# Fetched rows treated one by one, from dot to diagonal, outside the attention heads and the tanh units

## The chip, the cores and the metric

The kernel runs on one core of a Trainium2 chip. The metric is device microseconds of one execution. TensorE multiplies, VectorE and ScalarE work elementwise and reduce, GpSimd issues the gathers and SyncE the plain transfers; each engine works through its own list in order and waits on semaphores for the others.

## What is computed

Two blocks of a language model over 256 tokens of width 1024, in float32. The change is in the second block, whose two layers each end in a PEER feed-forward. It picks, for every token, 8 heads x 16 experts of 16384, and reads for each pick a row u and a row v:

```python
def peer_ffn(h, w_q, sub_keys, u_tab, v_tab):
    ...
    eidx = (i1 * PEER_NKEYS + i2).reshape(T, PEER_HEADS * PEER_TOPK)
    gates = jax.nn.softmax(cv, axis=-1).reshape(T, PEER_HEADS * PEER_TOPK)
    ...
        uc = jnp.take(u_tab, ic, axis=0)
        vc = jnp.take(v_tab, ic, axis=0)
        act = jax.nn.gelu(jnp.einsum('cd,ckd->ck', xc, uc).astype(jnp.float32))
        return jnp.einsum('ck,ckd->cd', (gc * act).astype(vc.dtype), vc)
```

Around it stand an LRU block, a stick-breaking attention with 16 heads, a per-layer embedding and norms. The first block (dilated attention, 32 experts of 2048 columns) comes before all that.

## The kernel before

The first 1165 us or so are the first block and the LRU block, most of it a stream of expert weights. Then the **row stage** begins. Layer by layer and token tile by token tile (128 tokens) it runs four **phases** f = 0 to 3: the PEER of layer 0 for tiles 0 and 1, then of layer 1 for both. A phase is 128 fetched "rows": row k holds, for each of the 128 tokens (one per partition), the u and v vectors of its k-th pick, 2 x 1024 floats, 1.05 MB in all. A phase has 64 **ticks** t of SHARE = 2 rows, a unit is one head of one tile (16 rows, 8 ticks).

The way of a row, with the lines of the profile:

- GpSimd issues its gather (L2701) into one of 8 buffers (9 from row 168 on), after it waited until TensorE had used the row that lay there before (`rows_used`). Indices come from the choice of the unit (`idx_ready`).
- VectorE multiplies u with the token vector in PSUM and sums (the dot, L2483), when the row has landed.
- ScalarE applies Gelu to the dots of the tick (L1871; in units 3 and 4 of phases 1 and 2 a Tanh form instead, L1869, `by_tanh`).
- VectorE multiplies it with the softmax factor into coefficients (L2510, tanh form L2507).
- ScalarE scales an identity by each coefficient into a diagonal (L1877, 8 slots).
- TensorE multiplies the diagonals with v into PSUM (`picks`, L1357) and so frees the row.

On every engine a tick is followed by a piece of other work, `chain(f - 1, t)`: the rest of the layer for the tile before (merging the sums at t = 0, squares, roots and scaled copies at t = 1 and 8, a gate with Sigmoid at 6 and 7, keys and values from 9, queries from 17, the attention heads from t = 22 to 38, the output projection from MERGE = 39, the questions to the next PEER from 45). Between dot and coefficient VectorE also runs pieces of the choice of later units (`choose`, L2412 to L2458), four to a unit: two top-16 searches of keys, one of pairs, and the row numbers. After a unit's last piece ScalarE computes an Exp for it (L1857). Gelu, Exp, Sqrt and Sigmoid each need other tables on ScalarE, so between them stands an ACT_TABLE_LOAD.

In `parts(f, t)` the two rows of a tick go together: two dots, then one Gelu over both, one coefficient instruction over both, two diagonals. Only in the last tick of all do they go one by one.

Of the kernel before, what the change touches and what calls it, by code (L numbers as in the profile page):

```python
# [35 lines left out]
TT = T // P  # L36
# [32 lines left out]
SHARE = 2  # L69
SHARES = PTOP // SHARE  # L70
PHASES = 2 * TT
PHASE = PH * PTOP
TICKS = PHASE // SHARE
# [10 lines left out]
HEADS, GROUP, GROUPS = 22, 4, HEADS2 // 4  # L84
SOFT, LOGS, MASKED, SUMS, ARGUE, EXPS, CAUSAL, WEIGH, KEEP = 1, 2, 3, 3, 5, 5, 6, 6, 7
MERGE, ADD3, SQUARE3, SCALE3, TURN3, GAIN3 = 39, 43, 43, 44, 44, 45
# [4 lines left out]
LAST, LAST_PROJ = PHASES - 1, 40  # L91
# [78 lines left out]
def row_buffer(k):  # L170

    return k % ROWS if k < MORE_AT else (k - MORE_AT + ROWS) % (ROWS + MORE_ROWS)
# [7 lines left out]
def chosen(f, t):  # L180

    if f == 0:
        return [FIRST_CHOICES[t]] if t in FIRST_CHOICES else []
    now = [(PH * f + 2 + j // 4, j % 4) for j in range(24) if int(1.75 * j) == t]
    if f < PHASES - 1 and CHOOSE <= t < CHOOSE + 8:
        now.append((PH * (f + 1) + (t - CHOOSE) // 4, (t - CHOOSE) % 4))
    return now
# [6 lines left out]

def parts(f, t):

    return range(SHARE) if (f, t) == (LAST, TICKS - 1) else range(0, SHARE, SHARE)


def by_tanh(f, t):  # L200

    return 1 <= f <= TT and t // SHARES in TANH_UNITS


class Tally:
# [6 lines left out]
    def mark(self, ins):  # L212
        ins.then_inc(self.sem, 1)
        self.n += 1
        return self.n
# [4 lines left out]
    def link(self, ins):  # L220
        self.mark(ins)
        self.wait()
# [9 lines left out]
def program(nc, io, out):  # L232
    first = plan()
    slot, slot_loads, freed_by = ring_plan(first)
    with ExitStack() as ctx:
# [187 lines left out]
        def rows(n):  # L423

            b = row_buffer(n)
            if b < ROWS:
                return big[:, b * ROW:(b + 1) * ROW]
            return ring[:, CHAIN_RING:RING, :].rearrange("p k d -> p (k d)")

        def diagonal(n):  # L430

            return diag_at[:, n % DIAGS * SIDE:(n % DIAGS + 1) * SIDE]
# [9 lines left out]
        def tok_bank(f):  # L442

            return (6, 0, 2, 0)[f]
# [1047 lines left out]
        def _(act):  # L1492
# [366 lines left out]

            def share(f, t):  # L1860

                for i, begin in enumerate(parts(f, t)):
                    n = f * TICKS + t + i
                    k = (f * TICKS + t) * SHARE + begin
                    size = SHARE // len(parts(f, t))
                    act.wait_ge(S["dots_ready"], n + 1)
                    at = slice(k % PICKS, k % PICKS + size)
                    if by_tanh(f, t):
                        act.activation(acts[:, at], g_arg, ACT.Tanh, scale=GELU_SLOPE).then_inc(S["gelu_ready"], 1)  # L1869
                    else:  # L1870
                        act.activation(acts[:, at], dots[:, at], ACT.Gelu_apprx_tanh, scale=1.0 if f else r_tok)\  # L1871
                            .then_inc(S["gelu_ready"], 1)
                    act.wait_ge(S["coef_ready"], n + 1)
                    for k in range(k, k + size):
                        if k >= DIAGS:
                            act.wait_ge(S["rows_used"], k + 1 - DIAGS)
                        act.activation(diagonal(k), fold, ACT.Copy, scale=coef[:, k % PICKS:k % PICKS + 1])\  # L1877
                            .then_inc(S["diags_ready"], 1)
# [7 lines left out]
            for f in range(PHASES):  # L1886
                for t in range(TICKS):
                    share(f, t)
                    if f == 0 and SECOND_CHOICE.get(t) == 2:
                        exps(1)  # L1890
# [33 lines left out]
        def _(dve):  # L1924
# [64 lines left out]
            for g, w in enumerate(POOL_WINDOWS):  # L1989
                s = (s0, s1)[g % 2][:, g, PAD:E]  # L1990
# [469 lines left out]
            def choose(n, piece):  # L2460
                if piece < 2:
                    best_keys(n, piece)
                elif piece == 2:
                    best_pairs(n)
                else:
                    rows_of(n)

            def share(f, t):

                u = f * PH + t // SHARES  # L2470
                u16 = u % UNITS
                if t == 0:
                    dve.wait_ge(S["tok_ready"], f + 1)
                tok = ps[:, tok_bank(f):tok_bank(f) + 2, :].rearrange("p b d -> p (b d)")
                for i, begin in enumerate(parts(f, t)):
                    n = f * TICKS + t + i
                    first_row = (f * TICKS + t) * SHARE + begin
                    size = SHARE // len(parts(f, t))
                    at = slice(first_row % PICKS, first_row % PICKS + size)
                    for k in range(first_row, first_row + size):  # L2480
                        dve.wait_ge(rows_loaded[row_buffer(k)], 16 * ROW_COUNT[k])
                        r = rows(k)[:, 0:D]
                        ins = dve.scalar_tensor_tensor(r, r, 1.0, tok, op0=ALU.mult, op1=ALU.mult,  # L2483
                                                       accum_out=dots[:, k % PICKS:k % PICKS + 1])
                        if by_tanh(f, t):
                            mark(ins)
                    if by_tanh(f, t):
                        step.wait()
                        link(dve.scalar_tensor_tensor(g_arg, dots[:, at], GELU_CUBE, dots[:, at], op0=ALU.mult, op1=ALU.mult))
                        dve.scalar_tensor_tensor(g_arg, g_arg, 1.0, dots[:, at], op0=ALU.add, op1=ALU.mult)\  # L2490
                            .then_inc(S["dots_ready"], 1)
                    else:
                        ins.then_inc(S["dots_ready"], 1)
                    if t % SHARES == 0:
                        dve.wait_ge(S["cv_exp"], u + 1)
                        link(dve.reciprocal(p_rec[:, u16:u16 + 1], p_sum[:, u16:u16 + 1]))
                        if by_tanh(f, t):
                            link(dve.tensor_scalar(p_rec[:, u16:u16 + 1], p_rec[:, u16:u16 + 1], 0.5, None, ALU.mult))
                    if by_tanh(f, t):
                        mark(dve.scalar_tensor_tensor(g_rest, dots[:, at], p_rec[:, u16:u16 + 1], cv[:, at],  # L2500
                                                      op0=ALU.mult, op1=ALU.mult))
                    for which, piece in chosen(f, t):
                        choose(which, piece)
                    dve.wait_ge(S["gelu_ready"], n + 1)
                    if by_tanh(f, t):
                        step.wait()
                        dve.scalar_tensor_tensor(coef[:, at], acts[:, at], 1.0, g_rest, op0=ALU.add, op1=ALU.mult)\  # L2507
                            .then_inc(S["coef_ready"], 1)
                    else:
                        dve.scalar_tensor_tensor(coef[:, at], acts[:, at], p_rec[:, u16:u16 + 1], cv[:, at],  # L2510
                                                 op0=ALU.mult, op1=ALU.mult).then_inc(S["coef_ready"], 1)
# [143 lines left out]
            for f in range(PHASES):  # L2655
                for t in range(TICKS):
                    share(f, t)
                    if f == 0 and t in SECOND_CHOICE:
                        choose(1, SECOND_CHOICE[t])
                    if f == 0 and t == ADD_NEXT:  # L2660
                        add_recurrent(1)
                    if f == 0 and t == SUM_NEXT:
                        sum_blocks(FFN + 1)
                    if f == 0 and t == NORM_NEXT:
                        tile_norm(FFN + 1, lambda c: col("norm_ffn", c))
                    if f == LAST and t == LAST_MERGE:
                        keep_sums(f)
                    if f:
                        chain(f - 1, t)
# [101 lines left out]
```

## Time and profile before

| | us |
|---|---|
| median of 3 runs | 2641.99 (2637.86 to 2642.75) |
| profiled execution | 2641.29 |
| its span, first to last instruction | 2639.1 |
| TensorE busy | 2149.6 |
| VectorE busy | 1362.4 |
| ScalarE busy | 633.1 |
| GpSimd busy | 492.7 |

The span holds 33067 instructions and 1053.60 MB of DMA, on average 399 GB/s; the gathers of the row stage are 540.07 MB of it. In the groups below, a time after a bar is idle time of the engine before those instructions, with what ended it; in the timelines it stands in brackets.

### The profile page before, as it was taken

Reading aid. Unit: us, or ns where it says so; the run is one execution under the profiler, and the core shown is the slowest. Engines: PE = TensorE matmul, PEld = TensorE weight load, DVE = VectorE, ACT = ScalarE, POOL = GpSimd, SP = SyncE. Lnnn points to the kernel's source line nnn. Section 1 sums busy time; section 2 is a strip of 40 time slices with the busy share of each in tenths; the row PEclk is TensorE's granted clock in tenths of the full one; section 3 lists DMA queues with packets and bytes.
Section 4 is the critical chain, followed back from the end, with each engine's and each line's share of the span. In section 5 each row is a group of like instructions: output and inputs, shape, how many; then the busy total and the mean of one; then the engine's idle time right before and its main releaser. Section 6 shows DMA issues by size and latency. Waiting matters only on the chain.

```text
span 2639.1 us, 33067 instructions
## 1 busy us (share of the span) xinstructions
PE 2149.6 (81%) x12087; PEld 954.9 (36%) x12087; DVE 1362.4 (52%) x3702; ACT 633.1 (24%) x1521; POOL 492.7 (19%) x534
## 2 busy tenths in 40 slices
PE   8999999999999999997765579577678677565557
PEld 6633333333333334994421123125123235121112
DVE  3422222122222123777677777874675875587754
ACT  0411111111111111342222242431332442232212
POOL 1000000000000000013333333332333332233331
PEclk9999999999999999999987789889799899687789
DMA  7899999999999999859999999999999999999995
GB/s 254 357 407 429 429 428 429 428 425 430 428 429 429 428 428 372 292 196 414 420 419 421 420 419 393 420 419 417 420 419 417 405 400 417 419 402 421 421 421 226
DMA packets 134409, 1053.60 MB, mean 399 GB/s; under 512 B 15601, under 2 KB 16025, under 8 KB 44177
## 3 DMA queue, kind: packets, MB, share of 16 engines
q0 software_dynamic: 75104, 540.07, 49.7%
q1 hardware_dynamic: 59184, 511.98, 47.0%
q8 instruction: 70, 1.15, 0.2%
q14 instruction: 51, 0.41, 0.0%
HBM read 1050.92 MB, written 2.63 MB: 399 GB/s over the span
## 4 chain that ended last, share of the span: by engine, by line
PE 41%; DMA 39%; DVE 13%; ACT 3%; issue 3%; POOL 1%; SPq 0%; DVEq 0%; POOLq 0%; ACTq 0%
DMA big<-in_uv,small 22%; PE ps L884 15%; DMA big<-in_w_gate_up 14%; PE ps L1357 7%; DVE big L2483 5%; PE ps L1049 3%; PE ps L1161 3%; DMA ring<-in_uv,small 2%; PE ps L926 2%; PE ps L1175 2%; PE ps L867 1%; PE ps L712 1%; ACT small L1877 1%; DVE small L2416 1%; DVE small L2413 1%
## 5 line engine op out<-in xcount | busy, mean ns | idle before, releaser
L1357 PE MATMUL ps<-big,small 64*64 64x512 f32 x3776 | 595.6, 741 | 389.8 <-ACT small L1877 385.7
L2701 POOL DMA_INDIRECT big<-in_uv,small x473 | 445.3, 941 | 1987.4 <-DVE small L2458 1109.4
L2483 DVE SCALAR_TENSOR_TENSOR big<-big,ps 128x1024 f32<-128x1024 f32 x473 | 569.5, 1218 | 265.1 <-DMA big<-in_uv,small 259.9
L884 PE MATMUL ps<-big 128*64 128x512 f32 x2304 | 525.6, 599 | 26.2 <-DMA big<-in_w_gate_up 23.9
L1357 PEld LDWEIGHTS ps<-big,small 64*64 64x64 f32 x3776 | 148.1, 157 | 758.3 <-ACT small L1877 560.8
L884 PEld LDWEIGHTS ps<-big 128*64 128x64 f32 x2304 | 156.0, 137 | 333.3 <-issue 288.5
L1877 ACT ACTIVATE small<-small 128x64 f32<-128x64 f32 x512 | 150.3, 340 | 299.5 <-DVE small L2510 242.1
L2160 DVE COPY big<-ps 128x512 f32<-128x512 f32 x32 | 22.1, 692 | 381.3 <-PE ps L884 381.3
L1871 ACT ACTIVATE small<-small 128x2 f32<-128x2 f32 (+1 forms) x225 | 51.7, 230 | 593.8 <-DVE big L2483 513.8
L2146 DVE TENSOR_TENSOR big<-ps,big 128x256 f32<-128x256 f32 x64 | 27.2, 425 | 299.5 <-PE ps L908 299.5
L1049 PEld LDWEIGHTS ps<-hs,ring 128*128 128x128 f32 x1152 | 131.7, 193 | 17.9 <-issue 16.0
L1049 PE MATMUL ps<-hs,ring 128*128 128x128 f32 x1152 | 136.3, 278 | 0.0
L884 PE MATMUL ps<-ring,big 128*64 128x512 f32 x512 | 121.1, 600 | 9.3 <-DMA ring<-in_w_gate_up 8.1
L2510 DVE SCALAR_TENSOR_TENSOR small<-small 128x2 f32<-128x2 f32 (+1 forms) x225 | 49.6, 221 | 81.9 <-ACT small L1871 76.7
L1583 ACT ACTIVATE big<-big 128x256 f32<-128x256 f32 x64 | 26.7, 416 | 228.8 <-DVE big L2147 228.8
L1357 PE MATMUL ps<-ring,small 64*64 64x512 f32 x312 | 53.7, 743 | 32.8 <-ACT small L1877 32.7
L1591 ACT COPY big<-ps 128x512 f32<-128x512 f32 x32 | 18.7, 585 | 250.8 <-PE ps L884 250.8
L1161 PE MATMUL ps<-ring,xT 128*128 128x512 f32 x152 | 70.6, 606 | 0.1
L1303 PEld LDWEIGHTS ps<-xT,ring 128*128 128x128 f32 x512 | 60.1, 196 | 13.7 <-issue 11.3
L926 PE MATMUL ps<-small,big 64*128 64x256 f32 x512 | 63.9, 389 | 0.0
L1571 ACT COPY big<-ps 128x512 f32<-128x512 f32 x32 | 18.7, 585 | 188.1 <-PE ps L884 188.1
L1303 PE MATMUL ps<-xT,ring 128*128 128x128 f32 x512 | 63.2, 283 | 0.5 <-DMA ring<-in_peer_w_q 0.5
(403 smaller groups left out, 2300.4 us busy)
## 6 DMA issues: line engine op xcount, KB each, us to landing
big<-in_w_gate_up SPq DMA_DIRECT2D x80, 2048.0 KB, 22.7
big<-in_w_down SPq DMA_DIRECT2D x64, 2048.0 KB, 24.1
ring<-in_w_gate_up SPq DMA_DIRECT2D x32, 2048.0 KB, 26.2
hs<-in_w_gate_up SPq DMA_DIRECT2D x16, 2048.0 KB, 26.1
ring<-in_peer_w_q SPq DMA_DIRECT2D x48, 512.0 KB, 9.8
ring<-in_ple_w_gate SPq DMA_DIRECT2D x22, 512.0 KB
ring<-in_w_in SPq DMA_DIRECT2D x16, 512.0 KB, 8.1
ring<-in_a_w_in SPq DMA_DIRECT2D x16, 512.0 KB, 5.0
```

What stands on the lines that cost most here:

```text
L884: last = pe.matmul(ps[side * CAP:(side + 1) * CAP, bank + b, :], o, w[:, at:at + BANK], start=start, stop=stop, skip_group_check=True)
L926: last = pe.matmul(half(G_OUT, side * DT // 2 + c), m_y[at, c * P:(c + 1) * P], m_gateT[at, :], start=False, stop=True, skip_group_check=True)
L1049: last = pe.matmul(ps[:, bank + e // 4, (e % 4) * P:(e % 4 + 1) * P], w[:, e * P:(e + 1) * P], src(c)[:, tt * P:(tt + 1) * P], start=(c == ...
L1161: last = pe.matmul(ps[:, bank + z, :], src[:, blocks(c)], w[:, z * BANK:(z + 1) * BANK], start=(c == 0), stop=(c == DT - 1), skip_group_ch ...
L1175: last = pe.matmul(ps[:, bank + half_, :], src[:, blocks(c)], w[:, half_ * BANK:(half_ + 1) * BANK], start=(c == 0), stop=(c == DT - 1), s ...
L1303: last = pe.matmul(ps[:, A + e // 4, blocks(e % 4)], w[:, blocks(e)], hd[:, blocks(c)], start=(c == 0 and e % 4 == 0), stop=(c == DT - 1), ...
L1357: last = pe.matmul(ps[tokens_ if by_halves else at, bank, :], diagonal(k)[tokens_, :], rows(k)[tokens_, D + z * BANK:D + (z + 1) * BANK], ...
L1871: act.activation(acts[:, at], dots[:, at], ACT.Gelu_apprx_tanh, scale=1.0 if f else r_tok)\
L1877: act.activation(diagonal(k), fold, ACT.Copy, scale=coef[:, k % PICKS:k % PICKS + 1])\
L2483: ins = dve.scalar_tensor_tensor(r, r, 1.0, tok, op0=ALU.mult, op1=ALU.mult, accum_out=dots[:, k % PICKS:k % PICKS + 1])
L2510: dve.scalar_tensor_tensor(coef[:, at], acts[:, at], p_rec[:, u16:u16 + 1], cv[:, at], op0=ALU.mult, op1=ALU.mult).then_inc(S["coef_ready" ...
L2701: pool.indirect_dma_start(out=rows(k), out_offset=None, in_=io[f"uv{n // UNITS}"], in_offset=bass.IndirectOffsetOnAxis(ap=rows_at[:, at:at ...
```

## The change

`parts` gives single rows in every tick, except in the two places where it still gives a pair: the tanh units (ticks 24 to 39 of phases 1 and 2) and the ticks of the attention heads (22 to 38 of the same phases). So 36 ticks stay paired, and 219 that were paired are split (the last was split before). In a split tick the order on VectorE is dot, wait for the Gelu, coefficient, dot, pieces of choosing, wait for the Gelu, coefficient; the reciprocal of a unit's sum goes with its first row. ScalarE does Gelu and diagonal for one row, then for the other. The counters behind `dots_ready`, `gelu_ready` and `coef_ready` are now counted by `parts_before`.

```diff
 def parts(f, t):
 
-    return range(SHARE) if (f, t) == (LAST, TICKS - 1) else range(0, SHARE, SHARE)
+    alone = (f, t) == (LAST, TICKS - 1) or not (by_tanh(f, t) or 1 <= f <= TT and HEADS <= t < MERGE)
+    return range(SHARE) if alone else range(0, SHARE, SHARE)
...
+def parts_before(f, t):
+
+    return sum(len(parts(g, s)) for g in range(f + 1) for s in range(t if g == f else TICKS))
...
+                done = parts_before(f, t)
                 for i, begin in enumerate(parts(f, t)):
-                    n = f * TICKS + t + i
+                    n = done + i
...
-                    if t % SHARES == 0:
+                    if t % SHARES == 0 and i == 0:
                         dve.wait_ge(S["cv_exp"], u + 1)
                         link(dve.reciprocal(p_rec[:, u16:u16 + 1], p_sum[:, u16:u16 + 1]))
...
-                    for which, piece in chosen(f, t):
+                    for which, piece in chosen(f, t) if i == len(parts(f, t)) - 1 else ():
                         choose(which, piece)
                     dve.wait_ge(S["gelu_ready"], n + 1)
```

The `done` lines stand in `share` of ScalarE and of VectorE alike. DMA, GpSimd and TensorE code is not touched.

## Rows read from the trace of the kernel before

**Rows 1.** The page: busy time per engine, and GB/s in 40 slices of the span.

```profile
PE 2149.6 (81%) x12087; PEld 954.9 (36%) x12087; DVE 1362.4 (52%) x3702; ACT 633.1 (24%) x1521; POOL 492.7 (19%) x534
...
GB/s 254 357 407 429 429 428 429 428 425 430 428 429 429 428 428 372 292 196 414 420 419 421 420 419 393 420 419 417 420 419 417 405 400 417 419 402 421 421 421 226
```

**Rows 2.** Windows: length, busy us of the engines, TensorE clock, DMA share, GB/s.

```profile
1595.00:1630.00 35.00, 35.00 (x158) 13.13 (x155) 20.78 (x58) 9.36 (x25) 12.96 (x15) 1.00 0.96 371
2065.00:2160.00 95.00, 72.10 (x468) 29.61 (x468) 80.34 (x219) 40.83 (x86) 32.48 (x35) 0.91 0.99 396
2310.00:2355.00 45.00, 32.58 (x172) 10.57 (x174) 37.67 (x102) 18.76 (x44) 16.17 (x18) 0.92 1.00 392
```

**Rows 3.** Chain of waits, 1570 to 1650: start, length, what.

```profile
1595.37 3.63 PE ps L1175 x8
1599.00 1.88 PE ps L1357 x16
```

**Rows 4.** Groups of VectorE, ticks 1 to 16 of phase 3: busy, mean ns, idle before.

```profile
L2483 DVE SCALAR_TENSOR_TENSOR big<-big,ps 128x1024 f32<-128x1024 f32 x29 | 34.3, 1215 | 0.0
L2510 DVE SCALAR_TENSOR_TENSOR small<-small 128x2 f32<-128x2 f32 x16 | 3.7, 231 | 9.3 <-ACT small L1871 9.2
```

**Rows 5.** The dots' groups, windows 1247.5:1515.6, 1542.5:1580.3, 1922.1:1960.4, 2377.6:2508.7 (two).

```profile
L2483 DVE SCALAR_TENSOR_TENSOR big<-big,ps 128x1024 f32<-128x1024 f32 x102 | 123.2, 1218 | 56.9 <-DMA big<-in_uv,small 55.3 <-issue 1.3
...
L2483 DVE SCALAR_TENSOR_TENSOR big<-big,ps 128x1024 f32<-128x1024 f32 x10 | 12.2, 1219 | 11.4 <-DMA big<-in_uv,small 11.4
...
L2483 DVE SCALAR_TENSOR_TENSOR big<-big,ps 128x1024 f32<-128x1024 f32 x11 | 13.3, 1217 | 9.8 <-DMA big<-in_uv,small 7.2 <-issue 2.5
...
L2483 DVE SCALAR_TENSOR_TENSOR big<-big,ps 128x1024 f32<-128x1024 f32 x46 | 55.7, 1218 | 18.0 <-DMA big<-in_uv,small 17.9
...
L2483 DVE SCALAR_TENSOR_TENSOR ring<-ring,ps 128x1024 f32<-128x1024 f32 x6 | 7.3, 1218 | 3.3 <-DMA ring<-in_uv,small 3.3
```

**Rows 6.** Timeline of VectorE, a bare tick: start, length, operation.

```profile
2345.79 1.22 DVE L2483 SCALAR_TENSOR_TENSOR ring<-ring,ps 128x1024 f32<-128x1024 f32 x1
...
2346.93 1.22 DVE L2483 SCALAR_TENSOR_TENSOR big<-big,ps 128x1024 f32<-128x1024 f32 x1
...
2348.56 1.21 DVE L2483 SCALAR_TENSOR_TENSOR big<-big,ps 128x1024 f32<-128x1024 f32 x1
```

**Rows 7.** Timeline of VectorE, ScalarE, the tick after an Exp (phase 3, tick 6).

```profile
2325.11 1.21 DVE L2483 SCALAR_TENSOR_TENSOR big<-big,ps 128x1024 f32<-128x1024 f32 x1
...
2329.23 0.22 DVE L2510 SCALAR_TENSOR_TENSOR small<-small 128x2 f32<-128x2 f32 x1 [1.76 <-ACT small L1871]
...
2327.70 1.28 ACT L1871 ACT_TABLE_LOAD   x1
```

**Rows 8.** Timeline of VectorE and ScalarE, tick 1 of phase 3.

```profile
2302.27 1.21 DVE L2483 SCALAR_TENSOR_TENSOR big<-big,ps 128x1024 f32<-128x1024 f32 x1
...
2306.78 0.22 DVE L2510 SCALAR_TENSOR_TENSOR small<-small 128x2 f32<-128x2 f32 x1 [0.56 <-ACT small L1871]
...
2306.46 0.20 ACT L1871 ACTIVATE small<-small 128x2 f32<-128x2 f32 x1
```

**Rows 9.** Timeline of TensorE, the two rows of tick 0 of phase 3.

```profile
2295.64 1.98 PE L1357 MATMUL ps<-ring,small 64*64 64x512 f32 x8 [4.65 <-ACT small L1877]
2297.37 1.96 PE L1357 MATMUL ps<-big,small 64*64 64x512 f32 x8
```

**Rows 10.** Timeline of VectorE, the coefficient of tick 7 of phase 3.

```profile
2336.83 0.22 DVE L2510 SCALAR_TENSOR_TENSOR small<-small 128x2 f32<-128x2 f32 x1 [3.51 <-ACT small L1871]
```

**Rows 11.** Timelines of GpSimd and VectorE: fetch and dot of rows 419, 161.

```profile
2368.20 0.94 POOL L2701 DMA_INDIRECT big<-in_uv,small  x1 [0.82 <-PE ps L1357]
...
2380.09 1.22 DVE L2483 SCALAR_TENSOR_TENSOR big<-big,ps 128x1024 f32<-128x1024 f32 x1 [1.26 <-DMA big<-in_uv,small]
...
1602.36 0.94 POOL L2701 DMA_INDIRECT big<-in_uv,small  x1 [0.30 <-issue]
...
1611.22 1.22 DVE L2483 SCALAR_TENSOR_TENSOR big<-big,ps 128x1024 f32<-128x1024 f32 x1
```

More of the change, by code:

```diff
@@ L2474, in share @@
                 tok = ps[:, tok_bank(f):tok_bank(f) + 2, :].rearrange("p b d -> p (b d)")
+                done = parts_before(f, t)
                 for i, begin in enumerate(parts(f, t)):
-                    n = f * TICKS + t + i
+                    n = done + i
                     first_row = (f * TICKS + t) * SHARE + begin
```

## The prediction

> **What bounds the kernel now.** I read the page first, then the windows, then the waits of VectorE. TensorE is the busiest engine by its share and VectorE has half the span [rows 1], but the 40 slices say what sets the time: outside the stage change near slice 17 the DMA moves some 420 GB/s until the end [rows 1]. The second half reads 512 rows of 1.05 MB; while only they are read, one costs 1.05 MB / 421 GB/s = 2.49 us, a tick of two 4.98 us. So a change pays or costs only where the DMA runs dry. The windows show three such stretches [rows 2]: 1595:1630 at 371 GB/s, 2065:2160 at 396, 2310:2355 at 392. Against 420 they lose 35 x 49/420 = 4.1, 95 x 24/420 = 5.4 and 45 x 28/420 = 3.0 us, 12.5 in all: the most that a better flow of buffers could win. It runs dry because a row is fetched only when the buffer eight or nine rows back has been multiplied.
>
> The dry stretches have different limits. The first is TensorE: weights and rows alternate, 3.63 + 1.88 = 5.51 us for each tick with never a gap [rows 3]. The second lies in ticks 25 to 43 of phase 2, of which the change leaves 25 to 39 alone. The third is the start of phase 3, where VectorE never waits for a row in 16 ticks (idle before its dots 0.0, the 29 of [rows 4] and 3 more) but waits 9.3 us for ScalarE; those ticks take 75.2 us, 4.70 each. Elsewhere VectorE has room: ticks 13 to 63 of phase 0 hold 56.9 us of waiting for rows (1.1 a tick), ticks 17 to 42 of phase 3 hold 18.0 + 3.3 = 21.3 (0.82 a tick) [rows 5].
>
> **What the change adds to a tick.** The dots, the diagonals and the matmuls stay as many. Each of 219 ticks (256 less 36 paired ones and the last, already split) gains one Gelu and one coefficient, and VectorE, which works in order, now stands still for ScalarE after each row. The price is in one bare tick [rows 6]: dot to dot is 2348.56 - 2346.93 = 1.63 us when the Gelu and the coefficient lie between, and 1.14 when they don't (2346.93 - 2345.79). So **+0.49 us on VectorE**, choice or no choice: a piece of choosing covers only the second Gelu.
>
> After an Exp, ScalarE reloads its tables first: diagonals, load, Exp, load, Gelu [rows 7]. In the pair two dots cover part of it, and the coefficient comes 2329.23 - 2325.11 = 4.12 us after the first dot. Alone, ScalarE starts 0.24 sooner (one diagonal fewer), the first coefficient comes at 3.86, the second a dot and a Gelu later at 5.49: **+1.37**, one tick in seven. The Trainium skill (ScalarE: Activation LUTs, What ACT_TABLE_LOAD costs) gives 1283 ns for the load and 2.66 us for a switch with its drain; [rows 7] show the 1.28 and the coefficient already 1.53 after the load began, so no drain. By the page's figure these ticks would cost some 2.8 us more each; nothing below uses it.
>
> Ticks 1 and 8 of phases 1 to 3 are dearest: ScalarE squares a tile, loads Sqrt, loads Gelu, and its Gelu ends 4.39 us after the first dot started [rows 8]. Two dots and a piece of choosing hid all but 0.56. Alone, the first coefficient waits till 4.51, and the second dot and the choosing (the coefficient's 4.51 less those 0.56 and the first dot's 1.14: 2.8) follow it, the second coefficient at 7.48: **+2.97**. No DMA issue moves in any queue's order; GpSimd and SyncE keep theirs, and the DMA bytes are the same. Bounds for all this: below, the Gelus could be absorbed by waits for rows, 0; above, every addition in a stretch without such waits.
>
> **What it gives back.** The first row of a pair no longer waits for its fellow: it is freed a dot (1.14) and perhaps a choice (up to 3.1) sooner relative to VectorE. The second finds TensorE with one row less to do: 0.9 us at full clock, 1.7 where the granted clock is low, as at tick 0 of phase 3 (2297.37 - 2295.64 between the two rows [rows 9]). There the merge waits for both, so tick 1 starts about 1.85 us sooner. In steady flow this is nothing: the DMA is the limit.
>
> **Where it lands.** Phase 0: 0.49 a tick plus the dear ones is 0.62 on average, under the 1.1 of waiting; carried from tick to tick VectorE's delay stays under 2.5 us, and buffers go out earlier by as much: 0, bounds -1 and +2. Phase 2: ticks 5 to 9 wait 9.8 us for rows [rows 5] and swallow it; its dry stretch is in the paired ticks: 0, bounds 0 and +1.
>
> Phase 1, start: tick 1 costs 2.97, ticks 2 to 4 0.5 each; waits for rows, 11.4 us over ticks 5 to 9 [rows 5], take it back. Tick 8 again, then 9 and 10: VectorE's tick 10 ends 3.5 us late. The TensorE stretch after it starts less late, since one row of tick 10 is already multiplied (0.94 at full clock, half of 1.88) and the Gelu of the other hides under its choice: some +1.5, an estimate. From there each tick is 5.51 us of TensorE, with VectorE at 5.9 or less in front of it, so the delay stays. The DMA is dry there: **+1.5**, bounds 0 and +3.5.
>
> Phase 3, start: -1.85 at tick 0, +2.97 at tick 1, +0.5 in ticks 2 and 3; TensorE's stretch over ticks 3 to 5 starts 1.1 late. Tick 6 has the tables (+1.37). At tick 7 the coefficient waits 3.51 us for ScalarE's Sigmoids [rows 10]; the pair had both dots and a choice done by then, alone the second dot and the choice (2.9) come after it and tick 8 starts +5.0. Tick 8: +2.97, so +7.9 at tick 9. Four ticks of 0.49: +9.9 at tick 13, whose first row (number 410) is freed 9.5 late, and so row 419 is fetched 9.5 late. How much of this the DMA had in hand is in the lead from fetch to dot: 2368.20 to 2380.09 is 11.9 us for row 419; in the dry stretch of phase 1 one took 1602.36 to 1611.22 = 8.9 [rows 11]. So 3.0 was queue, and up to 6.5 is idle DMA; less, as that 8.9 had VectorE's dot before it back to back and the row may have lain there. I take **+5**, bounds +1 and +11 (the whole delay). After tick 16 VectorE needs 4.98 - 0.82 + 0.62 = 4.8 a tick, still under 4.98: it catches up slowly and costs nothing more. The tail, already row by row, gains at most 0.3.
>
> Sum: 1.5 + 5 + 0 + 0 - 0.3 = +6.2 us on the profiled execution's 2641.3 (span 2639.1, about 2 us around it): 2647.5; the median of the runs is 0.7 above that execution, so **2648**.
>
> **Rivals.** *Hidden* (0.2): the lead hides more and the earlier buffers pay for phase 1: 0 to +4, 2642 to 2646. For it: the DMA reads 1.01 busy around all three stretches [rows 2]. Against: the 75.2 us without one wait for a row [rows 4].
>
> *Faster* (0.12): rows freed singly refill the queue. Each dry stretch begins when the held buffers reach the limit; freed one row's read (2.49) sooner, it starts 2.5 later. In stretches one and three that is -5, with none of the VectorE delay: 2637; more than 12.5 can't come. It decides where tick 10 of phase 1 and tick 9 of phase 3 end no later than before. The Trainium skill (Perfetto Trace Analysis, Optimizing Scalar/DVE Operations) says as much: where these engines aren't saturated but cause bubbles elsewhere, breaking up instructions may let work finish sooner; the same section has grouping pay where an engine is saturated. By the busy share of 52% the first half would apply, by [rows 4] the second does at phase 3's start.
>
> *VectorE becomes the bound* (0.13): phase 3 never catches up until tick 43 and the whole 11 shows, phase 1 gives its 3.5 and phase 0 its 2: 2642 + 16.5 = 2658.
>
> *As forecast* (0.55): +3 to +10, 2645 to 2652.
>
> **Numbers.** 0.2% of this kernel, 5.3 us, is about what can be told from nothing. The forecast case lies above it some six times in ten (0.33) and the bound case adds 0.13: slower 0.46. Same: 0.2 and the forecast's other 0.22, 0.42. Faster 0.12. The range 2638 to 2658 leaves out most of the faster case and the upper half of the bound case, under 0.2; the likeliest case alone is 2645 to 2652.
>
> **What would show it.** Coefficients (L2510) about 444 instead of 225, at 0.22 us, and their wait for ScalarE from 77 us to over 150; the idle before dots falls by about the sum; first row's dot to second row's dot 1.63 in bare ticks. Tick 1 of phase 3 near 8.5 us long (was 5.5), tick 8 near 9. The window after 2310 drier than 392 GB/s and longer. Wrong if VectorE's late ticks leave that window's GB/s as it was, if TensorE's stretch in phase 1 starts on time, or if the granted clock moves with the finer matmuls.

## The result, and the profile after

The median of 11 runs after is 2647.43 us (2643.25 to 2652.68), beside 2640.22 us (2636.32 to 2642.75) for 11 runs of the kernel before. The ratio is 1.0028, 95% interval 1.002 to 1.0035: 7 us slower, where +6.2 and a time of 2648 were forecast. The profiled execution took 2644.37 us with a span of 2642.2; that is 3.1 below its kernel's median, while the profiled execution before (2641.29) is 1.1 above its own, so the two traces differ in length by less than the kernels do.

The page after: busy times, GB/s in 40 slices, and three groups (busy, mean ns | idle before them).

```profile
PE 2186.6 (83%) x12087; PEld 944.0 (36%) x12087; DVE 1399.7 (53%) x3921; ACT 706.1 (27%) x1740; POOL 495.0 (19%) x534
...
GB/s 261 366 427 428 429 428 428 428 421 429 428 429 429 429 428 368 256 225 419 421 420 421 421 415 384 421 419 417 421 417 409 408 406 417 418 368 414 421 421 236
...
L2491 DVE SCALAR_TENSOR_TENSOR big<-big,ps 128x1024 f32<-128x1024 f32 x473 | 573.3, 1216 | 132.2 <-DMA big<-in_uv,small 131.8
...
L1878 ACT ACTIVATE small<-small 128x1 f32<-128x1 f32 (+1 forms) x444 | 101.9, 230 | 477.7 <-DVE big L2491 438.4
...
L2518 DVE SCALAR_TENSOR_TENSOR small<-small 128x1 f32<-128x1 f32 (+1 forms) x444 | 97.3, 219 | 207.8 <-ACT small L1878 206.0
```

The dots' group of the page before, for its idle time.

```profile
L2483 DVE SCALAR_TENSOR_TENSOR big<-big,ps 128x1024 f32<-128x1024 f32 x473 | 569.5, 1218 | 265.1 <-DMA big<-in_uv,small 259.9
```

Lines have moved: the dot is L2491 (was L2483), the coefficient L2518 (L2510), the Gelu L1878 (L1871), the diagonal L1884 (L1877), the multiplication with v L1363 (L1357), the gather L2709 (L2701). There are 219 more Gelus and coefficients, VectorE waits 206 us for ScalarE, and its idle time before the dots of this group has fallen by 132.9 us, which is 0.61 a split tick. Nearly all of that came out of waits for the DMA. In the GB/s line [rows 1] the slice that stands out is the 36th: 368 instead of 402.

Windows after (columns as in rows 2): TensorE's stretch of phase 1, phase 2's dry stretch, the start of phase 3, and a longer one of it.

```profile
1590.00:1625.00 35.00, 35.00 (x164) 13.01 (x166) 24.26 (x71) 11.01 (x31) 12.27 (x13) 1.00 0.95 353
2065.00:2160.00 95.00, 73.66 (x467) 30.20 (x457) 79.69 (x219) 42.35 (x88) 32.91 (x36) 0.89 1.00 402
2310.00:2355.00 45.00, 32.33 (x154) 9.63 (x152) 33.18 (x92) 19.88 (x47) 13.19 (x14) 0.84 0.90 341
2300.00:2400.00 100.00, 67.25 (x343) 18.52 (x341) 77.67 (x218) 38.09 (x100) 33.46 (x36) 0.81 0.96 381
```

Beside [rows 2] the first is drier (353 for 371; it is taken 5 us earlier, since the row stage begins 3.9 us earlier in this execution; the unchanged kernel traced again has 381 in the same window), the second is not (402 for 396), and the third is much drier: 341 for 392 (402 in that second trace). The groups of VectorE over ticks 1 to 16 of phase 3 after:

```profile
L2491 DVE SCALAR_TENSOR_TENSOR big<-big,ps 128x1024 f32<-128x1024 f32 x29 | 35.2, 1214 | 0.0
L2518 DVE SCALAR_TENSOR_TENSOR small<-small 128x1 f32<-128x1 f32 x32 | 7.0, 218 | 19.6 <-ACT small L1878 19.5
```

Still no wait for a row, and 19.6 us of waiting for ScalarE where [rows 4] have 9.3. The ticks take 88.9 us (2298.76 to 2387.67) where they took 75.3 (2302.27 to 2377.60), 13.6 more: 10.3 of it is this wait, 3.3 the 16 more coefficients.

Timelines of phase 3 after: TensorE in tick 0, then VectorE's dots and coefficients in ticks 1 and 2, 6 and 7, 8 and 9, then fetch and dot of row 419.

```profile
2290.54 1.98 PE L1363 MATMUL ps<-ring,small 64*64 64x512 f32 x8 [1.65 <-ACT small L1884]
...
2294.14 1.98 PE L1363 MATMUL ps<-big,small 64*64 64x512 f32 x8 [1.62 <-ACT small L1884]
...
2298.76 1.21 DVE L2491 SCALAR_TENSOR_TENSOR big<-big,ps 128x1024 f32<-128x1024 f32 x1
...
2303.18 0.22 DVE L2518 SCALAR_TENSOR_TENSOR small<-small 128x1 f32<-128x1 f32 x1 [3.20 <-ACT small L1878]
2303.32 1.22 DVE L2491 SCALAR_TENSOR_TENSOR big<-big,ps 128x1024 f32<-128x1024 f32 x1
...
2306.16 0.22 DVE L2518 SCALAR_TENSOR_TENSOR small<-small 128x1 f32<-128x1 f32 x1
...
2307.15 1.21 DVE L2491 SCALAR_TENSOR_TENSOR big<-big,ps 128x1024 f32<-128x1024 f32 x1
...
2326.51 1.21 DVE L2491 SCALAR_TENSOR_TENSOR big<-big,ps 128x1024 f32<-128x1024 f32 x1
...
2330.23 0.22 DVE L2518 SCALAR_TENSOR_TENSOR small<-small 128x1 f32<-128x1 f32 x1 [2.51 <-ACT small L1878]
...
2332.00 1.21 DVE L2491 SCALAR_TENSOR_TENSOR big<-big,ps 128x1024 f32<-128x1024 f32 x1
...
2336.41 0.22 DVE L2518 SCALAR_TENSOR_TENSOR small<-small 128x1 f32<-128x1 f32 x1 [3.19 <-ACT small L1878]
...
2342.17 1.21 DVE L2491 SCALAR_TENSOR_TENSOR big<-big,ps 128x1024 f32<-128x1024 f32 x1
...
2346.67 0.22 DVE L2518 SCALAR_TENSOR_TENSOR small<-small 128x1 f32<-128x1 f32 x1 [3.20 <-ACT small L1878]
...
2351.31 1.21 DVE L2491 SCALAR_TENSOR_TENSOR ring<-ring,ps 128x1024 f32<-128x1024 f32 x1
...
2352.94 1.22 DVE L2491 SCALAR_TENSOR_TENSOR big<-big,ps 128x1024 f32<-128x1024 f32 x1
...
2354.57 1.22 DVE L2491 SCALAR_TENSOR_TENSOR big<-big,ps 128x1024 f32<-128x1024 f32 x1
...
2376.30 0.94 POOL L2709 DMA_INDIRECT big<-in_uv,small  x1 [3.82 <-PE ps L1363]
...
2389.30 1.21 DVE L2491 SCALAR_TENSOR_TENSOR big<-big,ps 128x1024 f32<-128x1024 f32 x1
```

Read as lengths: tick 1 takes 2307.15 - 2298.76 = 8.39 us, tick 8 2351.31 - 2342.17 = 9.14, a bare dot, Gelu and coefficient 2354.57 - 2352.94 = 1.63. Row 419 is fetched at 2376.30, 8.1 later on the span's own clock than in [rows 11].

To say where the time lies, the table gives the length of each phase from its first dot to that of the next (phase 3: to the last row's dot), read from each trace, and the run's ratio to the kernel before. Each trace is one execution. The same code run again differs by up to 1 us a phase here, but phase 3 with the same split ticks has 324.8 in one trace and 326.6 in another, and phase 2 untouched has 393.2 and 395.1: differences under 2 us between two traces tell little. (Phase 3 wholly in pairs is steadier: 321.6 to 322.1 in three traces.) The time ahead of the row stage varies more: its first dot stands between 1169.3 and 1178.0 us in the 14 traces.

| kernel | split ticks | phase 0 | 1 | 2 | 3 | ratio (95%) |
|---|---|---|---|---|---|---|
| before | 0 | 342.3 | 380.0 | 393.7 | 322.1 | |
| e5_same_code | 0 | 341.4 | 379.7 | 393.2 | 321.7 | 1.0 (0.9991 to 1.0009) |
| after | 219 | 343.3 | 380.9 | 394.6 | 326.6 | 1.0028 (1.002 to 1.0035) |
| e1_phase0 | phase 0 | 343.0 | 377.6 | 395.1 | 321.6 | 1.0008 (0.9999 to 1.0017) |
| e2_phase3 | phase 3 | 341.9 | 379.0 | 393.0 | 324.8 | 1.0014 (1.0005 to 1.0023) |
| e3_not_starts | 168 | 343.2 | 377.6 | 394.2 | 321.8 | 1.0006 (0.9997 to 1.0015) |
| e4_coefs_last | 219, other order | 342.6 | 379.9 | 394.2 | 321.7 | 1.002 (1.001 to 1.0031) |
| e6_coefs_last_again | the same | 341.7 | 380.6 | 395.1 | 322.1 | 1.0015 (1.0006 to 1.0024) |
| e7_phase3_1to8 | phase 3, 1 to 8 | 341.2 | 380.0 | 393.6 | 329.6 | 1.0025 (1.0016 to 1.0034) |
| e9_p3_dots_first | the same, other order | 341.5 | 379.0 | 392.9 | 322.1 | 0.9999 (0.999 to 1.0008) |
| e11_p3_0to8 | phase 3, 0 to 8 | 342.3 | 379.0 | 393.8 | 326.9 | 1.001 (1.0 to 1.0021) |
| e10_p3_from_tick9 | phase 3, from 9 | 342.3 | 379.1 | 393.7 | 321.9 | 1.0005 (0.9995 to 1.0014) |
| e12_tick0_9to16 | 0, 9 to 16 of phases 1 to 3 | 341.8 | 379.4 | 394.2 | 320.3 | 0.9998 (0.9989 to 1.0007) |
| e8_coef_first | none | 341.9 | 379.2 | 393.4 | 321.3 | 1.0002 (0.9993 to 1.0011) |

### The profile page after: what moved, and what is told of

It is laid out like the page before. It is cut to its first block, busy times and chain, and to the rows that moved or that the text cites. A ratio compares the mean times of both kernels' runs of the same rounds, so it can differ in the third digit from the quotient of the medians.

```text
span 2642.2 us, 33727 instructions
## 1 busy us (share of the span) xinstructions
PE 2186.6 (83%) x12087; PEld 944.0 (36%) x12087; DVE 1399.7 (53%) x3921; ACT 706.1 (27%) x1740; POOL 495.0 (19%) x534
## 4 chain that ended last, share of the span: by engine, by line
PE 39%; DMA 32%; DVE 20%; ACT 6%; issue 2%; POOL 0%; SPq 0%; DVEq 0%; POOLq 0%; ACTq 0%
DMA big<-in_uv,small 17%; PE ps L890 15%; DMA big<-in_w_gate_up 14%; DVE big L2491 8%; PE ps L1363 5%; PE ps L1055 4%; PE ps L932 2%; PE ps L1181 2%; PE ps L1167 1%; DVE small L2518 1%; PE ps L1309 1%; PE ps L873 1%; ACT L1878 1%; PE ps L718 1%; PE ps L1126 1%
## 5 line engine op out<-in xcount | busy, mean ns | idle before, releaser
L1363 PE MATMUL ps<-big,small 64*64 64x512 f32 x3776 | 619.6, 747 | 347.4 <-ACT small L1884 347.0
L2709 POOL DMA_INDIRECT big<-in_uv,small x473 | 447.8, 947 | 1978.7 <-DVE small L2465 1104.2
L2491 DVE SCALAR_TENSOR_TENSOR big<-big,ps 128x1024 f32<-128x1024 f32 x473 | 573.3, 1216 | 132.2 <-DMA big<-in_uv,small 131.8
L1363 PEld LDWEIGHTS ps<-big,small 64*64 64x64 f32 x3776 | 129.3, 153 | 764.1 <-ACT small L1884 670.3
L1884 ACT ACTIVATE small<-small 128x64 f32<-128x64 f32 x512 | 174.2, 347 | 374.0 <-DVE small L2518 327.8
L1878 ACT ACTIVATE small<-small 128x1 f32<-128x1 f32 (+1 forms) x444 | 101.9, 230 | 477.7 <-DVE big L2491 438.4
L2518 DVE SCALAR_TENSOR_TENSOR small<-small 128x1 f32<-128x1 f32 (+1 forms) x444 | 97.3, 219 | 207.8 <-ACT small L1878 206.0
L1363 PE MATMUL ps<-ring,small 64*64 64x512 f32 x312 | 58.6, 807 | 33.8 <-ACT small L1884 33.8
```

Of the source, the lines that this page charges most:

```text
L1363: last = pe.matmul(ps[tokens_ if by_halves else at, bank, :], diagonal(k)[tokens_, :], rows(k)[tokens_, D + z * BANK:D + (z + 1) * BANK], ...
L2709: pool.indirect_dma_start(out=rows(k), out_offset=None, in_=io[f"uv{n // UNITS}"], in_offset=bass.IndirectOffsetOnAxis(ap=rows_at[:, at:at ...
```

## The experiments

All are edits of the changed kernel, most of them of the one line that says where rows are alone; the last one edits the kernel before.

**Which phases pay.** Phase 0 alone, phase 3 alone, and all of it without ticks 0 to 16 of phases 1 to 3:

```diff
-    alone = (f, t) == (LAST, TICKS - 1) or not (by_tanh(f, t) or 1 <= f <= TT and HEADS <= t < MERGE)
+    alone = (f, t) == (LAST, TICKS - 1) or f == 0
...
+    alone = (f, t) == (LAST, TICKS - 1) or f == LAST
...
+    alone = (f, t) == (LAST, TICKS - 1) or (f == 0 or t > 16) and not (by_tanh(f, t) or 1 <= f <= TT and HEADS <= t < MERGE)
```

> Only phase 0 (64 ticks) and the last tick are split, the others stay paired. My theory: phase 0 has 1.1 us of waiting for rows in each tick and swallows 0.62, so 0, within -1 to +2 us of the kernel before. Rival (each split tick costs its share of the whole, 7.2 us over 219 ticks): +2.1 us. Rival (earlier buffers pay): faster by 1 us or more.

2641.59 beside 2639.37 us. The ratio's interval (-0.3 to +4.5 us) holds 0 and the +2.1 of an equal share alike, so this run alone doesn't decide.

> Only phase 3 (64 ticks) is split. My theory: its start, where the DMA is already dry, carries most of the loss, so +5 us (+3 to +7), and the window after 2310 moves fewer GB/s than 392. Rival (equal share per tick): +2.1 us.

2642.19 us, 2.8 above before in median, 3.7 by the ratio of 1.0014, at the low end of +3 to +7; phase 3 is 3.1 longer than in the control, and the window 2310:2355 has 365 GB/s. The interval (1.3 to 6.1 us) holds the rival's +2.1 too, so this run doesn't exclude an equal share; the next and e7_phase3_1to8 do.

> Split as in the changed kernel, but ticks 0 to 16 of phases 1 to 3 stay paired: 168 of the 219 ticks are still split. My theory: the loss sits in the starts, so within 1.5 us of the kernel before. Rival (equal share per tick): +5.5 us.

2640.59 us, 1.2 over before in median (1.6 by the ratio, at most 4.0 by its interval) with three quarters of the split ticks still there; an equal share would have been +5.5. So the 51 ticks at the starts carry most of the price. The chain of waits shows it at phase 1. After, the last piece ahead of TensorE's alternating pieces (weights 3.63, rows 1.88), and the first of these:

```profile
1585.21 1.09 PE ps L1363 x8
1586.30 3.63 PE ps L1181 x8
1589.93 1.88 PE ps L1363 x16
```

And in e3_not_starts:

```profile
1580.38 1.95 PE ps L1363 x16
1582.33 3.63 PE ps L1181 x8
1585.96 1.88 PE ps L1363 x16
```

And in the kernel before, in its first trace and in e5_same_code (a second one, below):

```profile
1588.79 4.69 PE ps L1175 x8
```

```profile
1586.33 3.63 PE ps L1175 x8
```

The row stage begins at 1169.5 after and at 1169.3 in e3_not_starts, and the pieces have one length. Counted from there the stretch starts 3.8 us later with the start of phase 1 split, and ends as late: phase 1 is 380.9 and 377.6 long. The kernel before lies between them. With its row stage at 1173.4 and 1171.8 its stretch starts 415.4 and 414.5 us in, beside 416.8 after and 413.0 in e3_not_starts. So against the kernel before the stretch is 1.4 to 2.3 late.

**Is it the stall or the instructions?** Here the count of Gelus and coefficients stays that of the change, but the order in a split tick is: both dots, choice, both coefficients; ScalarE does both Gelus, then both diagonals.

```diff
+                    for k in range(k0, k0 + SHARE):
+                        dve.wait_ge(rows_loaded[row_buffer(k)], 16 * ROW_COUNT[k])
+                        r = rows(k)[:, 0:D]
+                        dve.scalar_tensor_tensor(r, r, 1.0, tok, op0=ALU.mult, op1=ALU.mult,
+                                                 accum_out=dots[:, k % PICKS:k % PICKS + 1]).then_inc(S["dots_ready"], 1)
...
+                    for which, piece in chosen(f, t):
+                        choose(which, piece)
+                    weigh(0)
+                    weigh(1)
```

> The same 219 ticks with one Gelu and one coefficient per row, but VectorE does both dots, then the choice, then both coefficients, and ScalarE both Gelus, then both diagonals: as many instructions as in the changed kernel, without the stall between the rows. My theory (the price is the stall of VectorE in order, 0.49 us of 0.49 in a bare tick and 2.97 in ticks 1 and 8, not the instruction): a tick costs some 0.15 us more than the pair's, so 0 to +1.5 us against the kernel before. Rival (the instructions themselves cost it): +5 to +8 us, like the changed kernel.

2643.2 beside 2639.37 us, ratio 1.002. The ranges asked for 0 to +1.5 or +5 to +8; it came between. Phase 3 is back at 321.7. To see whether the rest was real I ran it again beside the unchanged kernel:

> The kernel before, unchanged, as a control for times and for a second trace: ratio 1.000 within 0.1%, and the four phases within 1 us each of the first trace (342.3, 380.0, 393.7, 322.1 us from dot to dot). If the phases of this trace differ by 3 us or more, single traces can't carry a phase's cost.

> The kernel of e4_coefs_last again, with a fresh set of runs: there its median was 3.8 us above the kernel before, but its traced execution had the same length of row stage (1438.4 against 1438.1 us). If the stall is the price, 0 to +2 us; if the second Gelu and coefficient instructions are a price too, +3 us or more again, and then the trace should show where.

The control gives ratio 1.0 and phases within 0.9 us. The reordered kernel is again slower, 2642.1 beside 2638.62 us, 3.5. Its two traces are 2.4 and 3.5 us longer than the control's over four phases, but only 0.3 and 1.4 longer than the first trace of the kernel before, with nothing above 1.9 in any one phase and nothing in phase 3. So the order removes phase 3's price; what costs the rest, with every tick's instructions there but no stall between the dots, these runs don't say.

**The stall by itself.** Eight ticks in a row, the dearest among them, as the change has them, and with both dots first:

```diff
+    alone = (f, t) == (LAST, TICKS - 1) or f == LAST and 1 <= t <= 8
```

> Only ticks 1 to 8 of phase 3 are split (and the last tick): 8 of the 219. My theory: the delay of VectorE gathered there (2.97 in ticks 1 and 8, the wait at 7) makes most of phase 3's loss: +2 to +4 us on phase 3 in the trace, where e2_phase3 had +2.7. Rival (equal share): +0.3 us. Rival (the later ticks of the phase make the loss, by keeping VectorE behind): 0 to +1 us.

> Ticks 1 to 8 of phase 3 alone: one Gelu and one coefficient for each row as in the run that split these eight ticks (ratio 1.0025, phase 3 longer by 7.9 us than in the control), but both dots and the choice stand before both coefficients, so VectorE never stands still between the two dots. Same count of instructions, no stall. If the order (the stall for ScalarE) is the price there: phase 3 from its first dot to its last within 2 us of the control's 321.7, ratio 1.000 to 1.001. If the eight extra instructions of each engine are the price: 7 to 8 us again, ratio 1.0025.

This is the cleanest pair. e7_phase3_1to8 took 2645.54 beside 2638.62 us, phase 3 +7.9; I had expected +2 to +4. e9_p3_dots_first, with as many instructions, took 2639.88 beside 2639.34, phase 3 +0.4. VectorE's coefficients in ticks 1 to 8 (busy, mean ns | idle before them), in the control, then e7_phase3_1to8, then e9_p3_dots_first:

```profile
L2510 DVE SCALAR_TENSOR_TENSOR small<-small 128x2 f32<-128x2 f32 x8 | 1.9, 235 | 6.7 <-ACT small L1871 6.7
```

```profile
L2518 DVE SCALAR_TENSOR_TENSOR small<-small 128x1 f32<-128x1 f32 x16 | 3.5, 219 | 14.1 <-ACT small L1878 14.0
```

```profile
L2501 DVE SCALAR_TENSOR_TENSOR small<-small 128x1 f32<-128x1 f32 x16 | 3.0, 215 | 6.1 <-ACT small L1874 5.8
```

The wait for ScalarE goes from 6.7 to 14.1 and back to 6.1, and phase 3 from 321.7 to 329.6 and back to 322.1: 7.5 us between the last two, beside 8.0 us more of waiting. With the same number of instructions in both, the order is the cause. The windows 2300:2400 of the same three:

```profile
2300.00:2400.00 100.00, 68.08 (x369) 20.32 (x371) 83.32 (x224) 36.38 (x91) 37.65 (x40) 0.86 1.01 412
```

```profile
2300.00:2400.00 100.00, 63.73 (x336) 18.25 (x336) 78.53 (x213) 35.56 (x89) 34.38 (x36) 0.85 0.96 375
```

```profile
2300.00:2400.00 100.00, 67.08 (x376) 19.82 (x376) 83.39 (x224) 35.24 (x96) 38.08 (x41) 0.85 1.00 405
```

412 - 375 GB/s over 100 us, at 412, is 9.0 us of reading that wasn't done, for a phase 7.9 longer. (The windows stand at one place of the span, while phase 3 begins at 2286.1, 2287.3 and 2282.8.)

**What gives back.** But all of phase 3 split cost only 3.1 in its trace. Tick 0 was added to the eight, then everything from tick 9 tried alone, and last both kinds of places in phases 1 to 3:

```diff
+    alone = (f, t) == (LAST, TICKS - 1) or f == LAST and t <= 8
...
+    alone = (f, t) == (LAST, TICKS - 1) or f == LAST and t >= 9
...
+    alone = (f, t) == (LAST, TICKS - 1) or f >= 1 and (t == 0 or 9 <= t <= 16) and not (by_tanh(f, t) or 1 <= f <= TT and HEADS <= t < MERGE)
```

> Split in ticks 0 to 8 of phase 3. Beside the run with ticks 1 to 8 it adds only tick 0, where the merge waits for both rows: I had put this at 1.85 us given back on VectorE. Theory: phase 3 near 321.7 + 7.9 - 2 = 328, ratio 1.0015 to 1.002, the rest of what splitting all of phase 3 gave back (3.1 of 7.9 remained) being due to the ticks from 9 on. Rival (tick 0 is the whole of what was given back): phase 3 near 325, ratio 1.001.

2643.13 us, 3.8 over before in median (2.6 by the ratio) where e7_phase3_1to8 has 6.9; phase 3 326.9, between the 328 of the theory and the 325 of the rival. Tick 0 gives back 2.7 of the 7.9. The 2.1 between 326.9 and e2_phase3's 324.8 can't be put down to the ticks from 9 on, as the next table shows, and by the runs e2_phase3 is no cheaper: its ratio is 1.0014, this one's 1.001.

> Split only in phase 3 from tick 9 on, its start left in pairs. The theory (the eight ticks 1 to 8 put VectorE late, the ticks after them give part back, because rows are freed singly): phase 3 1 to 4 us shorter than the control's 321.7 us, or equal if the starts' delay is needed for there to be anything to give back; ratio 0.999 to 1.0005. Rival (every split tick costs its share, 54 ticks here of 219): +1.8 us, ratio 1.0007 and a longer phase 3.

2640.02 beside 2639.34 us; phase 3 321.9. No gain and no loss in the phase; that these ticks would shorten it by 1 to 4 by themselves is refuted. The interval of the ratio holds the rival's +1.8 us as well.

How late VectorE is within phase 3, in us against the control: the starts of the first dots of ticks 1, 9 and 17, counted from the phase's first dot, and the last row's dot (from unrounded starts, so a last digit can differ from the table above):

| kernel | split in phase 3 | tick 1 | 9 | 17 | last row |
|---|---|---|---|---|---|
| before | none | +0.9 | +0.9 | +0.4 | +0.4 |
| e7_phase3_1to8 | 1 to 8 | +0.9 | +10.0 | +9.2 | +7.9 |
| e11_p3_0to8 | 0 to 8 | -1.5 | +7.5 | +6.8 | +5.2 |
| e2_phase3 | all | -2.9 | +6.2 | +10.3 | +3.1 |
| after | all | -1.4 | +7.6 | +11.7 | +5.0 |
| e10_p3_from_tick9 | from 9 | -0.2 | -0.2 | +3.8 | +0.2 |
| e12_tick0_9to16 | 0, 9 to 16 | -1.1 | -0.5 | +3.6 | -1.3 |

e2_phase3 and e11_p3_0to8 run the same code up to tick 8, and two thirds of their 2.1 us are there at tick 1 already. From tick 9 to the last row the delay shrinks by 2.1 and 2.3 us with the later ticks in pairs, and by 3.1 and 2.6 with them alone: at most 1 us apart, less than two traces of one kernel can differ by. What single rows add in ticks 9 to 16, some 4 us, is gone at the end in each of the four rows that have them. What decides is how late tick 9 starts.

> A candidate: of phases 1 to 3 split only tick 0 and ticks 9 to 16, the places where the split seemed to give back and not to cost; 27 ticks in all. Theory (single rows free buffers sooner where VectorE does not fall behind): 2 to 4 us under the kernel before, ratio 0.9985 to 0.999. Rival (the give-back only repairs a delay that the split itself made): ratio 0.9995 to 1.0005. If the extra instructions cost wherever they stand: 27 of 219 ticks, +0.9 us, ratio 1.0003.

The candidate, the last line of the diff above: 2638.27 beside 2639.34 us, ratio 0.9998, with phases that sum to 0.3 less than the control's. The expected 2 to 4 us are not there, though the interval reaches from -2.9 to +1.8. Its phase 3, 320.3, is the shortest of all traces, 1.4 under the control's and there from tick 1 on, so it is not shown that tick 0 gives nothing where nothing is late.

**A gain from the other side.** In the kernel before, with pairs kept, a long piece of choosing was put behind the coefficient in eleven ticks of phases 1 to 3, so that rows are freed sooner:

```diff
-                    for which, piece in chosen(f, t):
+                    after = f and t in (3, 5, 10, 12, 17, 19, 24, 26, 31, 38, 40)
+                    for which, piece in () if after else chosen(f, t):
...
+                    for which, piece in chosen(f, t) if after else ():
+                        choose(which, piece)
```

> The kernel before with its pairs, but in ticks 3, 5, 10, 12, 17, 19, 24, 26, 31, 38 and 40 of phases 1 to 3 the long pieces of choosing (3.1 us) come after the coefficient instead of ahead of it. Each costs VectorE 0.3 us of waiting for the Gelu and frees both rows some 3 us sooner. If the DMA's dry stretches come from rows held too long, those of phases 2 and 3 (5.4 and 3.0 us) shrink: -3 to -5 us. If they come from VectorE's pace, +0.5 to +2 us.

2639.65 beside 2638.62 us, ratio 1.0002. My -3 to -5 was wrong (the interval ends at -1.8): freeing rows ahead of a choice gains nothing that these runs can tell.

## Why the prediction was right, and where it wasn't

The sign, the size and the mechanism came out; some terms inside did not, and that 6.2 met 7.2 so closely is in part luck, since errors of 1 to 2 us in phase 3 cancelled. (The prediction also puts the DMA at 1.01 busy around the dry stretches; in them [rows 2] show 0.96, 0.99 and 1.00.)

- **A bare tick, +0.49**: 1.63 us with a Gelu and a coefficient between two dots, as in [rows 6], and ticks 9 to 12 of phase 3 are 0.5 to 0.6 longer each. Over all split ticks the waits for rows of the group above shrank by 0.61 a tick, beside the mean of 0.62 forecast for phase 0.
- **After an Exp, +1.37**: tick 6 of phase 3 takes 5.49 us where it took 4.26, +1.23; the coefficient comes 2330.23 - 2326.51 = 3.72 after the dot (forecast 3.86).
- **Ticks 1 and 8, +2.97**: the first coefficient of tick 1 comes at 4.42 (forecast 4.51), the second at 7.40 (7.48); tick 1 is 2.9 longer, tick 8 3.0.
- **Tick 0, -1.85**: TensorE has the first row 3.6 us before the second, and tick 1's dot comes 10.5 us after tick 0's instead of 12.8: -2.3. The control has 12.0 and e2_phase3 9.1, so one trace can't size it better than by 1 us or so; e11 beside e7 puts its worth at 2.7.
- **Tick 7, +5.0 at tick 8**: this step was too dear. Tick 8's first dot stands 53.95 us (2342.17 - 2288.22) into the phase where it stood at 50.20 (2339.63 - 2289.43): +3.7. The 2.9 behind the coefficient came out. But the forecast's +5.0 has the coefficient 2.1 late, and it came at 2336.41, in [rows 10] at 2336.83: with the phase's first dot 1.2 earlier than before on the span's clock that is 0.8 late. The tick is as long as before (10.2 us), since the wait for the Sigmoids took up VectorE's earlier lateness. Before, ScalarE stood idle 2.74 us for TensorE ahead of them; after, it ran them with no wait behind their table load:

```profile
2334.12 1.08 ACT L1730 ACTIVATE big<-ps 128x512 f32<-128x512 f32 x2 [2.74 <-PE ps L1161]
```

```profile
2333.78 1.08 ACT L1736 ACTIVATE big<-ps 128x512 f32<-128x512 f32 x2
```

So tick 9 is at +6.7 (forecast 7.9), tick 13 at +8.7 (9.9), tick 17 at +11.3, all against the first trace.
- **Phase 3, +5 (+1 to +11)**: row 419 is fetched 8.1 + that 1.2 = 9.3 us late within the phase (forecast 9.5), the window is drier (341 GB/s), and the phase is 4.9 longer than the control's, 4.5 longer than before. Split alone it is 3.1. The eight ticks cost 7.9 and tick 0 gives back 2.7. I took the delay of tick 13 (+9.9), less 3.0 of queue, for the most that shows. The runs put it otherwise: the 2 us or so that ticks 9 to 12 add, and what 13 to 16 add, cost nothing in the end (e10_p3_from_tick9), and the delay at tick 9 less 2.1 to 3.1 us remains. So the 3.0 was about right, and a start 1.2 too late and ticks 9 to 12 at full price were made up for by taking +5 where the sum gave 6.5. How much was queue can't be read from row 419's own lead: after, it is 13.0 us (2376.30 to 2389.30), longer than the 11.9 before, since its dot waits for VectorE and not for the row.
- **Phase 1, +1.5 (0 to +3.5)**: about right. Against the kernel before the stretch starts 1.4 to 2.3 late and phase 1 is 0.9 to 1.2 longer; against e3_not_starts, where phase 0 is split as well, it is 3.8 and 3.3, at my upper bound. The relief for a row of tick 10 already multiplied is there: 8 matmuls (1.09 us) stand ahead of the stretch where e3_not_starts has 16 (1.95).
- **Phase 0, 0 (-1 to +2)**: wherever it is split it is 1.6 to 1.9 longer than in the control and 0.7 to 1.0 longer than in the first trace. Where the start of phase 1 is in pairs that phase is 2.1 shorter behind it, so the two together are as long as in the control (720.6 and 720.8 for 721.1); the time of the run alone is unresolved.
- **Phase 2, 0 (0 to +1)**: 394.6 beside 393.7 and the control's 393.2, within what two traces differ by; the dry window is at 402 for 396. Nothing speaks against the forecast.

The rival *hidden* falls with the drier window and phase 3's 4.9. *VectorE becomes the bound* falls too: of its 11.0 us at tick 16 less than half is left at the end. *Faster* falls with the measured time; its own sign, a tick 9 of phase 3 no later than before, is missed by 6.7 us, and e12_tick0_9to16 shows no such gain either. The Trainium skill (Perfetto Trace Analysis, Optimizing Scalar/DVE Operations) says that breaking up instructions may allow work to be completed sooner where these engines aren't saturated but cause bubbles elsewhere. Tick 0 is such a place, worth 2.7 us here; where the next dot stands behind the wait, the finer grain made the bubble.

## What to carry to other kernels

Before you split a batch on an engine that works in order, look at what stands behind the wait in its list: the price at the start of phase 3 was not the small extra instruction (16 of them cost nothing that could be measured; all 438 with both dots first cost 3.5 to 3.8 us in the median, outside phase 3 and unexplained) but the work that used to cover the other engine's latency and now waits for it. It is highest where that latency is longest, here behind table loads, and where the engine has no slack: eight ticks of 256 made a price as high as that of the whole change. Put all independent work ahead of the first wait. Don't count a sooner release as a gain before something waits for it: single rows from tick 9 on gained nothing that could be measured, with a delay ahead of them or without, while tick 0, where the merge waits for both rows, gained some 2.7 us ahead of one.

## What the runs showed of the hardware

I had named a moving granted clock as a sign of being wrong. It did move: its mean over the span was 0.904 to 0.912 in the 11 runs of the changed kernel, 0.921 on average in 33 runs of the kernel before, and 0.912 on average in e3_not_starts. That one has most of the fall for 1.2 us in the median, and e7_phase3_1to8 has 6.9 us at 0.918, which speaks against the lower clock as the source of the 7 us. In the start of phase 3 the window 2310:2355 has 0.84 where [rows 2] have 0.92, a larger part of it at 1.2 instead of 2.4 GHz; but e1_phase0, with phase 3 in pairs, has 0.85 there, so this window's clock can't be put down to the split. TensorE was busy for 32.3 of the 45 us and waited in the others. What makes the clock fall was not tried.
